# Four sets of token-quarter combinations in a split-precision FFN: which engine forms each, and when

## The reference, cut to what matters

```python
h2 = _rmsnorm(x, g_pre_ffn) * (1 + sc2) + sh2
up = _dwconv_rows(jnp.einsum('bld,df->blf', h2, w_up), conv_w, conv_b, grid)   # w_up: 1024 x 5632
ug, uv = jnp.split(up, 2, axis=-1)
f = jnp.einsum('blf,fd->bld', jax.nn.gelu(ug) * uv, w_down)
```

## Time and profile before

| what | value |
|---|---|
| median of the three runs | 1868.85 us |
| the profiled execution's own time | 1868.85 us |
| its span in the profile | 1866.5 us |
| TensorE busy in the span | 1832.8 us (98%) |
| VectorE, ScalarE, GpSimd busy | 1080.2, 711.8, 214.0 us |
| mean granted TensorE clock | 0.998 of full speed |

### The profile page before, as it was taken

One profiled execution on the slowest core, in us unless ns is written; L12 is line 12 of the kernel. 1 busy time (PEld: TensorE's weight loads), 2 busy tenths in 40 slices (PEclk: granted clock), 3 DMA queues, 4 the chain that ended last, 5 costly groups with the idle time before them and its releaser, 6 DMA issues.

```text
span 1866.5 us, 27369 instructions
## 1 busy us (share of the span) xinstructions
PE 1832.8 (98%) x10922; PEld 1714.4 (92%) x10922; DVE 1080.2 (58%) x2279; ACT 711.8 (38%) x1220; POOL 214.0 (11%) x232
## 2 busy tenths in 40 slices
PE   7999999999999999999999999999999999999997
PEld 2999999999999999999998899999999999888886
DVE  2663545545545544346364569777777777656563
ACT  3633321234232324254143454444444444443432
POOL 2000000000000010011000042222222221001111
PEclk9999999999999999999999999999999999999999
DMA  9133223323323353148232231333233234868682
GB/s 350 36 87 94 70 75 94 90 75 119 106 47 118 108 131 121 64 169 279 69 114 90 85 106 67 108 107 98 96 99 101 97 100 163 295 226 286 227 282 93
DMA packets 202563, 239.96 MB, mean 129 GB/s; under 512 B 9944, under 2 KB 162548, under 8 KB 202436
## 3 DMA queue, kind: packets, MB, share of 16 engines
q1 hardware_dynamic: 185204, 174.88, 29.8%
q0 software_dynamic: 12736, 45.56, 7.3%
q10 hardware_dynamic: 4496, 17.77, 2.3%
HBM read 180.50 MB, written 57.68 MB: 128 GB/s over the span
## 4 chain that ended last, share of the span: by engine, by line
PE 91%; DVE 4%; ACT 2%; DMA 1%; issue 1%; SPq 0%; ACTq 0%; POOL 0%; DVEq 0%; POOLq 0%
PE ps L1203 22%; PE ps L1231 14%; PE ps L886 13%; PE ps L888 13%; PE ps L887 13%; PE ps L1141 5%; PE ps L1022 2%; PE ps L1025 2%; PE ps L1024 1%; PE ps L928 1%; PE ps L1001 1%; DVE H_lo L1791 1%; DMA adaw<-in_w_ada_dram 1%; PE ps L913 1%; ACT Wt L1462 1%
## 5 line engine op out<-in xcount | busy, mean ns | idle before, releaser
L886 PE MATMUL ps<-H_hi,ring_hi 128*128 128x384 f32 x1416 | 491.3, 347 | 6.3 <-DVE H_lo L1791 4.4
L888 PE MATMUL ps<-H_hi,ring_lo 128*128 128x384 f32 x1416 | 474.6, 335 | 0.0
L887 PE MATMUL ps<-H_lo,ring_hi 128*128 128x384 f32 x1416 | 474.4, 335 | 0.0
L886 PEld LDWEIGHTS ps<-H_hi,ring_hi 128*128 128x128 f32 x1416 | 266.4, 188 | 10.3 <-DVE H_lo L1791 5.5
L887 PEld LDWEIGHTS ps<-H_lo,ring_hi 128*128 128x128 f32 x1416 | 266.6, 188 | 1.1
L888 PEld LDWEIGHTS ps<-H_hi,ring_lo 128*128 128x128 f32 x1416 | 266.1, 188 | 0.0
L1939 DVE SCALAR_TENSOR_TENSOR Cst<-Cst,Et,ps 128x257 f32<-128x257 f32 x64 | 30.9, 484 | 222.1 <-PE ps L1025 222.1
L1203 PE MATMUL ps<-T_lo,up_hi 128*128 128x288 f32 x608 | 130.3, 296 | 0.0
L1203 PE MATMUL ps<-T_hi,up_lo 128*128 128x288 f32 x608 | 130.2, 296 | 0.0
L1203 PE MATMUL ps<-T_hi,up_hi 128*128 128x288 f32 x608 | 130.2, 296 | 0.0
L1791 DVE TENSOR_TENSOR down_lo<-down_raw,down_hi 128x1024 fp32r<-128x1024 f32 x66 | 80.7, 1223 | 76.8 <-ACT f_hi L1699 76.8
(11 more groups left out here) (278 smaller groups left out, 3298.9 us busy)
## 6 DMA issues: line engine op xcount, KB each, us to landing
down_raw<-in_w_down_dram SPq DMA_DIRECT2D x66, 512.0 KB, 3.8
raw<-in_w_in_dram SPq DMA_DIRECT2D x44, 512.0 KB, 3.9
up_raw<-in_w_up_dram SPq DMA_DIRECT2D x38, 512.0 KB, 5.2
raw<-in_w_ada_dram SPq DMA_DIRECT2D x32, 512.0 KB, 4.9
f_raw<-z_gate SPq DMA_DIRECT2D x66, 192.0 KB, 3.6
v_raw<-z_value SPq DMA_DIRECT2D x66, 192.0 KB, 4.0
z_gate<-mid_g SPq DMA_DIRECT2D x38, 288.0 KB, 4.1
z_value<-mid_v SPq DMA_DIRECT2D x38, 288.0 KB, 4.7
```

The source lines that it names most:

```text
L886: pe.matmul(out, whi, xhi, start=first, stop=False)
L887: pe.matmul(out, whi, xlo, start=False, stop=False)
L888: return pe.matmul(out, wlo, xhi, start=False, stop=last)
```

## The change

GpSimd now runs sets 0, 1 and 2, with the four weight sums of pair 0 between set 0 and set 1; the weight sums of pairs 1 to 18 follow. VectorE runs only set 3, in one piece, between `plain_up(0)` and `plain_up(1)`. The table `between` and the pieces of `quarter_tiles` are gone. On ScalarE and VectorE the splits of sets 3 and 0 stand behind `plain_up(1)`, in that order; those of sets 1 and 2 stand behind `plain_up(2)` and behind weight splits 2 and 3 of pair 0. TensorE's program, the synchronous engine's transfers and all tiles are as they were.

```diff
+            for n, k in enumerate(range(KD // 2 - 1)):          # GpSimd
+                quarter_tiles(pool, pool_sums, k, 8 * n)
+                if n == 0:
+                    for j in range(4):
+                        weight_sum(0, j)
+            for s in range(1, NP):
-            for k in range(2):
-                quarter_tiles(pool, pool_sums, k, 8 * k)
-            for s in range(NP):
                 for j in range(4):
                     weight_sum(s, j)
...
             def quarter_split(k):                               # ScalarE
-                if k >= 2:
-                    act.wait_ge(dve_sums, 8 * (k - 1))
+                if k == KD // 2 - 1:
+                    act.wait_ge(dve_sums, 8)
                 else:
                     act.wait_ge(pool_sums, 8 * (k + 1))
...
-                    if f == 2 and half:
-                        quarter_split(3)
...
-            quarter_split(0)
             plain_up(1, [[4], [5]])
-            quarter_split(1)
+            for k in (KD // 2 - 1, 0):
+                quarter_split(k)
             up_hi_split(0, 0)
             up_hi_split(0, 1)
-            quarter_split(2)
             plain_up(2, [[], []])
-            for i in range(2, 6):
+            for i in (2, 3):
+                up_hi_split(0, i)
+            for k in range(1, KD // 2 - 1):
+                quarter_split(k)
+            for i in (4, 5):
                 up_hi_split(0, i)
...
-            def between(f, block):                              # VectorE
-                if (f, block) == (1, 1):
-                    quarter_split(0)
-                if (f, block) == (1, 2):
-                    quarter_tiles(dve, dve_sums, 2, 0, 0, 3)
...
             plain_up(0, [[2], [3]])
+            quarter_tiles(dve, dve_sums, KD // 2 - 1, 0)
             plain_up(1, [[4], [5]])
+            for n, k in enumerate((KD // 2 - 1, 0)):
+                quarter_split(k, n)
+            next_weights(-1, 0)
+            next_weights(-1, 1)
             plain_up(2, [[], []])
-            for i in range(2, 6):
+            for i in (2, 3):
+                next_weights(-1, i)
+            for k in range(1, KD // 2 - 1):
+                quarter_split(k, k + 1)
+            for i in (4, 5):
                 next_weights(-1, i)
```

More of the change, by code:

```diff
@@ L563, in free_slot, with quarter_tiles @@
             eng.wait_ge(ring_read, 1)
-    def quarter_tiles(eng, done, k, before, lo=0, hi=8):
+    def quarter_tiles(eng, done, k, before):
         first, second = slice(0, HT), slice(HT, T)
@@ L576, in quarter_tiles @@
         for n, (out, a, b, op) in enumerate(steps):
[L577 to L580, removed]
+            if n:
+                eng.wait_ge(done, before + n)
+            eng.tensor_tensor(out, a, b, op).then_inc(done, 1)
     with nc.Block() as block:
@@ L2106, in _ @@
             norm_split(NB * KD, tsc2, 2, NB - 1)
[L2109 to L2114, removed]
             def plain_up(f, splits):
@@ L2154, in plain_up, with quarter_split @@
                             ins.then_inc(conv_value_done, 1)
-                        between(f, NB * half + b)
                 assert n[0] == 8 * (f + 1)
+            def quarter_split(k, n):
+                dve.wait_ge(quarter_hi, n + 1)
+                for name in quarters:
+                    ins = sub_hi(T_lo[name][:, k, :], T_full[name][:, k, :], T_hi[name][:, k, :])
+                ins.then_inc(quarter_lo, 1)
             def up_lo_split(s, i):
@@ L2217, in next_weights @@
                     down_split(i - 2)
-            def between(f, block):
-                if (f, block) == (1, 1):
-                    quarter_split(0)
-                if (f, block) == (1, 2):
-                    quarter_tiles(dve, dve_sums, 2, 0, 0, 3)
[L2225 to L2241, removed]
             plain_up(0, [[2], [3]])
+            quarter_tiles(dve, dve_sums, KD // 2 - 1, 0)
             plain_up(1, [[4], [5]])
+            for n, k in enumerate((KD // 2 - 1, 0)):
+                quarter_split(k, n)
+            next_weights(-1, 0)
+            next_weights(-1, 1)
             plain_up(2, [[], []])
-            for i in range(2, 6):
+            for i in (2, 3):
[3 more added lines that the diff above has]
+            for i in (4, 5):
                 next_weights(-1, i)
```

## The result

The changed kernel took 1882.04 us (median of four runs, 1880.99 to 1883.66), the kernel before 1868.28 us (four runs, 1867.16 to 1869.04; the three of the table above had 1868.85). The ratio is 1.0075 with a 95% interval of 1.0057 to 1.0093: 13.8 us slower, where 14.05 were forecast (1882.9 us).

The account below looks back on a forecast made before the run. TensorE, busy 98% of the span, was taken to bound the kernel. A 12.35 us wait at product 2 plus 1.7 us for the clock, 14.05 us on 1868.85, gave 1882.9 us; range 1878.5 to 1887.

Parts of the forecast that it names:

- What leaves VectorE is worth nothing: VectorE loses eight sums of set 2; TensorE waits for none of its plain taps there, so worth 0.
- When GpSimd gets to set 1: Set 1, queued behind pair 0's four weight sums on GpSimd, starts at 1147.5 us instead of 1111.74.
- How long the sets take: GpSimd runs set 1 from 1147.5 to 1159.6 us and set 2 until 1173.4.
- The contention term: In set 2, some four GpSimd sums beside VectorE's subtractions take 0.4 us more each: 1.7 us.
- From the last sum to TensorE: After set 2's last sum, `T_hi` on ScalarE and `T_lo` on VectorE follow; product 2 starts at 1178.75 us.
- The wait: TensorE starts pair 0's product 2 12.35 us later than 1166.39, all of it idle.
- What is queued behind: Later weight copies, splits and pair 1's weight sums are late by the same 12 us; counted as 0.
- The clock: TensorE's clock falls to 1.2 GHz in the stall; about 3.4 us at half speed costs 1.7 us, ends 0 and 3.4.
- Full blocking: Shared SBUF port stops GpSimd's set 2 for six VectorE subtractions, 4.0 us instead of 1.7: 1885.2 us; chance 7%.
- The clock stays up: No clock loss after the stall at product 2, or clock back at once: 1881.2 us; chance 5%.
- A second wait: In pair 0 or 1 TensorE waits again for a weight or freed bank, 3.2 us: 1886.1 us; chance 5%.
- Not slower: GpSimd ends set 2 by 1161.2 us, set 1 starting by about 1135: 1868.85 us, at best 0.65 less; chance 5%.

Follow-up runs that it names:

- the changed kernel with a steady clock: Changed kernel with unused filler matmuls in TensorE's two short waits near 870 and 1096 us: 1882.72 us, ratio 1.0076 to the plain kernel before.
- the steady pair: Kernel before and changed kernel, both with unused filler matmuls in TensorE's short waits near 870 and 1096 us: 1868.22 and 1882.72 us.
- the same fillers: Unused matmuls in TensorE's short waits near 870 and 1096 us, no longer than the waits; added to the kernel before: 1868.22 us.
- the third kernel: Changed kernel with filler matmuls in the two short waits and 80 in the wait at product 2: 1879.65 us, ratio 1.0062 to the plain kernel before.
- the experiment without neighbours: Changed kernel with VectorE's `T_lo` of set 1 held back until GpSimd has ended set 2: 1882.71 us, ratio 1.0075 to the kernel before.
- the second experiment: Changed kernel with GpSimd's sets 0 to 2 in a row and splits of sets 1 and 2 ahead of `plain_up(2)`: 1870.59 us, ratio 1.0008.
- the first experiment: Changed kernel with GpSimd's sets 0, 1 and 2 in a row, pair 0's weight sums behind them: 1876.02 us, ratio 1.0032 to the kernel before.
- the fourth steady kernel: Changed kernel with GpSimd's three sets in a row and filler matmuls in the two short waits: 1873.01 us, ratio 1.0023 to the plain kernel before.

## Why the prediction was right, step by step

- **What leaves VectorE is worth nothing.** Right. VectorE's busy time between 1122 and 1160 us fell from 36.6 us to 23.1, and TensorE waits for it there neither before nor after.
- **When GpSimd gets to set 1.** Right in mechanism and size. Counted from set 0, the first weight sum came 32.65 us later (33.3 forecast), set 1 50.84 us later (forecast 1147.5 - 1098.08 = 49.4). The 1.4 us more are the fall of the clock at 1100 us, since ScalarE and VectorE here are paced by TensorE's blocks: in the changed kernel with a steady clock set 1 starts 49.30 us behind set 0 (1147.18 against 1097.88).
- **How long the sets take.** 11.9 and 14.1 us against 12.1 and 13.8. The contention term was 1.7 and measured 2.2 (14.1 less 11.9): six sums at 1.75 to 1.80 us, where four at 0.4 more were counted. That it is contention was shown by taking the neighbours away.
- **From the last sum to TensorE.** 1177.59 to 1182.87 is 5.28 us; forecast 5.35.
- **The wait.** 12.27 us longer (12.32 in the steady pair) against 12.35.
- **What is queued behind.** Right that nothing is added: with the wait filled and the clock up, product 2 to the end is 699.19 us, against 700.31 before with the same fillers. No second wait appeared. But it is 1.1 us shorter, which the forecast, with nothing behind product 2 to take any of the delay up, left out; 0.9 of it is the wait for `held_v`.
- **The clock.** Right that it falls, low in size: 1.7 forecast, 2.1 and 2.7 us in two profiles and 3.1 between medians. The step took over 3.4 us at half speed from another place; here half speed lasted 4.6 and 5.9 us after the work resumed. It stayed inside the bound of 3.4. Of the 3.1 between medians 2.7 are in the rows behind the wait, and some 0.4 can be the `held_v` wait, which only the third kernel lacks.
- **The rivals.** "Full blocking" failed for set 2 by the experiment without neighbours. It had only GpSimd stand still, while in set 2 VectorE was held for most of each GpSimd sum (1.9 us for a subtraction of 0.69). But the second experiment has a GpSimd instruction that was held for 5.35 us, so the rival was wrong on this set and not on what the two engines can do to each other. "The clock stays up" failed by the rows. "A second wait" did not occur. "Not slower" would have needed set 1 to start by about 1135; the first two experiments gave GpSimd that, and still paid 3.3 us until the splits were moved too. On that rival the prediction was incomplete: it took GpSimd's last sum as the single point of decision and did not say that the splits' place alone, behind the last value block, makes 3.3 us.

The forecast sum, 14.05 us, stands beside 13.8 in the first comparison and 14.5 in the steady one. The wait is right by its mechanism. That the total is as close owes something to luck: in the steady pair the clock cost 1.0 us more than forecast, and 0.5 us came back further on (12.32 + 2.7 - 0.5 = 14.5).

## What to carry to other kernels

An engine that is 12% busy is not free to take work: what counts is what stands ahead of the new work in its queue. Here four short sums, tied to another engine's progress, held two sets for 37 us (set 1 started 13.66 us behind set 0 before, and 50.84 now). Before moving work to an idle engine, write down when each instruction ahead of it is released, and then look for the second limit under the first, as it shows only when the first is gone. And a wait of the matmul engine costs more than its length: 2 to 3 us here for the clock.

## What the runs showed of the hardware that was not expected

Around waits of TensorE as short as 1.9 to 3.3 us its clock falls to 0.50 (1.2 GHz) in some executions and not in others. The fall can come when the work is already back: in the changed kernel's profile 0.4 us after the wait of 2.4 us near 870, and 1.5 us after that of 1.9 us near 1100. It lasted 3.4 us in both, 3.4 us in the first experiment behind a wait of 3.2 us, and 6.8 us in the fourth steady kernel behind a wait of the same length. The plain kernel before, with waits of 2.2 and 1.9 us near 870 and 1096 us, shows mean clocks from 0.996 to 0.998 and times from 1867.44 to 1871.31 us. With matmuls in those waits ten of eleven runs stand at 0.998. A difference of one or two us between kernels of this kind can be the clock's alone; distances between marks in the two traces show it where medians don't.

When a VectorE instruction with two sources in SBUF runs beside GpSimd's sums, both get slower, but not alike: from 1.43 to 1.8 us on GpSimd, from 0.76 to 1.87 on VectorE for the same 128x576 shape. That is how sets 1 and 2 went, GpSimd's sums in a row. It can go the other way: the weight sum of the second experiment took 6.96 us instead of 1.61, while VectorE's row of eight subtractions lost nothing. In both places the engine that was held had its instruction start while the other's row was running; that this decides it was not tested.
